# A two-block transformer kernel on one core: the gated-linear output projection and its layer norm turned to token rows, residual sums of the last projection on VectorE, two weight chunks moved in one pass

## The reference, cut to what matters

```
first_block:  x = x + g1 * rmsnorm(mixer(h));  h = rmsnorm(x)*(1+sc2)+sh2
              x = x + g2 * rmsnorm(conv_ffn(h))
layer 0:      y = (o * silu(g)) @ gla_w_out          # (256 x 1024) @ (1024 x 1024)
              x = layer_norm(ALPHA * x + y, ln_g[0], ln_b[0])
layer 1:      k, v = shared_kv(x);  y = dilated_mixer(x, k, v)    # ends with @ swa_w_out
              x = layer_norm(ALPHA * x + y, ln_g[1], ln_b[1])
```

## Time and profile before

| | us |
|---|---|
| median of three runs (785.42 to 787.11) | 786.86 |
| the profiled execution, its time | 786.95 |
| its span in the trace | 785.2 |
| PE busy, of the span | 751.5 (96%) |
| DVE busy | 528.7 (67%) |
| ACT busy | 394.9 (50%) |
| POOL busy | 121.3 (15%) |
| moved by the transfers, in all | 140.10 MB, mean 178 GB/s |

### The profile page before, as it was taken

One profiled execution on the slowest core, in us unless ns is written; L12 is line 12 of the kernel. 1 busy time (PEld: TensorE's weight loads), 2 busy tenths in 40 slices (PEclk: granted clock), 3 DMA queues, 4 the chain that ended last, 5 costly groups with the idle time before them and its releaser, 6 DMA issues. The chain is left out here.

```text
span 785.2 us, 14371 instructions
## 1 busy us (share of the span) xinstructions
PE 751.5 (96%) x6044; PEld 732.4 (93%) x6044; DVE 528.7 (67%) x770; ACT 394.9 (50%) x555; POOL 121.3 (15%) x100
## 2 busy tenths in 40 slices
PE   8899989999898999999999999999989999999996
PEld 7889889899897999999999999999989999999995
DVE  5879978765868687778656556926685556556544
ACT  4195454555353555454444347627445555555633
POOL 0040000000521100000002150000025655333000
PEclk9999999999999999999999999979999999999999
DMA  8975575464355356554565524523437653333101
GB/s 355 417 291 215 215 268 187 190 259 171 108 177 199 115 208 210 173 200 157 209 247 210 211 90 180 184 88 108 145 124 246 201 185 135 134 109 119 44 1 54
DMA packets 20954, 140.10 MB, mean 178 GB/s; under 512 B 2357, under 2 KB 2997, under 8 KB 4890
## 3 DMA queue, kind: packets, MB, share of 16 engines
q1 hardware_dynamic: 20458, 137.28, 48.2%
q0 software_dynamic: 432, 1.90, 0.7%
HBM read 138.12 MB, written 1.05 MB: 177 GB/s over the span
## 5 line engine op out<-in xcount | busy, mean ns | idle before, releaser
L1593 PE MATMUL res<-hhi,whi 128*128 128x256 f32 (+1 forms) x1120 | 322.9, 288 | 5.3 <-DVE hlo L1071 2.9
L1035 DVE TENSOR_TENSOR wlo<-raw,whi 128x2048 fp32r<-128x2048 f32 (+3 forms) x102 | 230.0, 2256 | 142.9 <-ACT whi L647 138.3
L1595 PE MATMUL res<-hlo,whi 128*128 128x256 f32 (+1 forms) x1120 | 317.8, 284 | 0.0
L1594 PE MATMUL res<-hhi,wlo 128*128 128x256 f32 (+1 forms) x1120 | 317.8, 284 | 0.0
L647 ACT ACTIVATE whi<-raw 128x2048 fp32r<-128x2048 f32 (+3 forms) x102 | 190.1, 1865 | 132.5 <-issue 100.2
L1593 PEld LDWEIGHTS res<-hhi,whi 128*128 128x128 f32 (+1 forms) x1120 | 214.6, 192 | 7.2 <-issue 5.5
L1594 PEld LDWEIGHTS res<-hhi,wlo 128*128 128x128 f32 (+1 forms) x1120 | 214.4, 191 | 0.3
L1595 PEld LDWEIGHTS res<-hlo,whi 128*128 128x128 f32 (+1 forms) x1120 | 214.3, 191 | 0.2
L559 POOL TENSOR_TENSOR sq<-sq 128x512 f32<-128x512 f32 x6 | 14.9, 2482 | 293.7 <-ACT sq L853 168.5
L1593 PE MATMUL res<-uhi,whi 128*128 128x256 f32 x176 | 49.3, 280 | 1.0 <-ACT y L854 1.0
L1594 PE MATMUL res<-uhi,wlo 128*128 128x256 f32 x176 | 49.2, 280 | 0.0
(11 more groups left out here) (331 smaller groups left out, 1242.0 us busy)
## 6 DMA issues: line engine op xcount, KB each, us to landing
raw<-in_wts SPq DMA_DIRECT2D x97, 1024.0 KB, 4.9
raw<-in_w_ada SPq DMA_DIRECT2D x16, 1024.0 KB, 4.9
shared<-in_w_ada SPq DMA_DIRECT2D x6, 1024.0 KB, 12.6
gates<-in_wts SPq DMA_DIRECT2D x3, 1024.0 KB, 15.4
raw<-in_wts SPq DMA_DIRECT2D x4, 768.0 KB, 7.3
y<-in_w_ada SPq DMA_DIRECT2D x2, 1024.0 KB, 10.3
x<-in_xT SPq DMA_DIRECT2D x2, 512.0 KB, 4.5
ln_rows<-in_ln_rows POOLq DMA_DIRECT2D x1, 1024.0 KB, 7.9
```

Of the source, the lines that this page charges most:

```text
L1035: nc.vector.tensor_tensor(lo[:, 0:b], raw[RAW_OF["w", c] % RAW][:, 0:b], hi[:, 0:b].bitcast(f32), ALU.subtract).then_inc(lo_ready, 1)
L1593: mm(out, ah, bh, start=first, stop=False)
L1594: mm(out, al, bh, start=False, stop=False)
L1595: return mm(out, ah, bl, start=False, stop=last)
```

## The change

1. The output projection of the gated-linear layer is token-major. `GOUT` is one narrow product for both halves of the tokens; then for each half t of 128 tokens comes a wide product, in which the stationary activations stay and the 512 columns of two chunks (`GOUT+1`, `GOUT+2`, slots 0 and 2 of one `whi` tensor) move in one pass, and a narrow one (`GOUT+3`, split into a buffer of its own, `wgo`). PE adds the residual from `xe` by identity matmuls.
2. The norm n5 is made on rows (`rows_centred`, `rows_scaled`), and PE then turns the rows back (`hidden(t)`: 8 transposes). ACT and DVE split them into `hhi`, `hlo` (`hidden_high`, `hidden_low`). `SK` and `SK+1` are then products of their own (`fm`) in place of one interleaved `fm_first`. POOL loads `ln_rows5` (1 MB).
3. The last projection: wide product for `SOUT`, `SOUT+1`; `SOUT+2` and `SOUT+3` in quarter results; the residual is added by DVE as it reads the result (`row_add`), PE's identity matmuls there are gone.
4. n2, n3, n4: all additions to `x` on DVE, `ada` of `UP` after the n2 additions in place of ahead of them, `load_root()` earlier on ACT (at `WOUT+2` and `DOWN`), in n4 the low parts are made between the additions, and 24 fillers in place of 36.

```diff
@@ ACT
                 if b not in LATE and b not in (GOUT + 1, GOUT + 2) and b != WOUT + 2 and b >= DIRECT:
                     high(c + 2)
...
+                if b == DOWN:
+                    load_root()
...
                     if j == 2:
+                        load_root()
                         high(c + 2)
...
+                if b == GOUT + 3:
+                    row_sum(result(FIRST_RESULT[b])[:, :], 1, T, 512, 1).then_inc(drained_act, 1)
+                    act.wait_ge(z_shift, 2)
+                    row_squares(z[:, 1, 0:768], 1, 0, 3).then_inc(z_squared, 1)
+                    hidden_high(0)
+                    high(SK)
+                    ps = result(FIRST_RESULT[b] + 1)[:, 0:T]
+                    row_sum(ps, 1, 768, T, 2).then_inc(z_summed, 1)
+                    row_squares(ps, 1, 768, 4).then_inc(drained_act, 1)
+                    row_root(1, 0)
+                    hidden_high(1)
+                    high(SK + 1)
@@ DVE, n2 and n4
-                            if i == 1 and k % 2:
-                                ins.then_inc(y_scaled[n], 1)
-                            else:
-                                own(ins)
-                        if i != 1:
-                            nc.vector.tensor_tensor(x[:, 2 * j:2 * j + 2, :], x[:, 2 * j:2 * j + 2, :],
-                                                    y[:, 2 * j:2 * j + 2, :], ALU.add).then_inc(scaled[n], 1)
-                        if n == "n4" and i == 2:
-                            low_pair(0)
+                            own(ins)
+                        if n == "n4" and i:
+                            low_pair(i - 1)
+                        nc.vector.tensor_tensor(x[:, 2 * j:2 * j + 2, :], x[:, 2 * j:2 * j + 2, :],
+                                                y[:, 2 * j:2 * j + 2, :], ALU.add).then_inc(scaled[n], 1)
                     if n == "n4":
-                        for i in (1, 2, 3):
-                            low_pair(i)
+                        low_pair(3)
                 if b == UP - 1:
+                    ada(ADA_AFTER[UP])
@@ DVE, the rows
+                if b == GOUT + 3:
+                    dve.wait_ge(drained_act, RESULT_DRAIN[FIRST_RESULT[b]][1])
+                    shift_of(1)
+                    hidden_low(0)
+                    low(SK)
+                    rows_centred(1, 0, gv)
+                    rows_scaled(1, 0, gv, x_rows, x_rows_ready)
+                    hidden_low(1)
+                    low(SK + 1)
...
+                def row_add(ps, t, a, n, at):
+                    return nc.vector.tensor_tensor_reduce(out=z[:, t, a:a + n], in0=ps, in1=x_rows[:, t, a:a + n], op0=ALU.add,
+                                                          op1=ALU.add, scale=1.0, scalar=0.0, accum_out=zs[:, t, at:at + 1])
@@ PE
-                        warm(36)
+                        warm(24)
...
+            def wide_product(ps, t, k, ih, il, slots, first, last):
+                wh, wl = (h[:, slots, k * T:k * T + T] for h in (whi, wlo))
+                return three(ps[:, :].rearrange("p (s n) -> p s n", s=2), ih[:, k, t * P:t * P + P], il[:, k, t * P:t * P + P],
+                             wh, wl, first, last)
...
+                    if c == GOUT:
+                        pe.wait_ge(xe_ready, 1)
+                        ps = bank(r)
+                        for t in range(2):
+                            residual(ps, T * t, t, (0, 1))
+                        wh, wl = weights(c)
+                        for k in range(KT):
+                            pe.wait_ge(go_lo, k // 2 + 1)
+                            for t in range(2):
+                                last = token_product(ps, T * t, t, k, gohi, golo, wh, wl, False, k == KT - 1 and t == 1)
+                        last.then_inc(product_done, 1)
+                    if c == GOUT + 1:
+                        for t in range(2):
+                            ps = bank(r + 1 + 2 * t)
+                            residual(ps, 0, t, range(2, 6))
+                            wait_weights(GOUT + 2)
+                            for k in range(KT):
+                                last = wide_product(ps, t, k, gohi, golo, slice(0, 3, 2), False, k == KT - 1)
+                            last.then_inc(product_done, 1)
+                            if t == 1:
+                                hidden(0)
+                            ps = bank(r + 2 + 2 * t)
+                            residual(ps, 0, t, (6, 7))
+                            wh, wl = weights(GOUT + 3)
+                            for k in range(KT):
+                                last = token_product(ps, 0, t, k, gohi, golo, wh, wl, False, k == KT - 1)
+                            last.then_inc(product_done, 1)
+                        warm(16, ident, pX[:, 0:P])
+                        hidden(1)
```

More of the change, by code:

```diff
@@ L102, in drainer_of @@
         return "dve"
-    if GOUT <= c < SV or SWA <= c < SWA + 12:
+    if SK <= c < SV or SWA <= c < SWA + 12 or c >= SOUT:
         return "dve"
@@ L130 @@
     CHUNK_MARK.append(_m)
+CHUNK_MARK[GOUT + 1] = RESULT_MARK[FIRST_RESULT[GOUT + 3]]
+CHUNK_MARK[GOUT + 2] = CHUNK_MARK[GOUT + 1]
 STREAM = []
@@ L197, in laid_out @@
     if c < SK:
-        return cols(gla_out, 256 * (c - GOUT), 256)
+        return cols(gla_out, (0, 512, 256, 768)[c - GOUT], 256)
     if c < SWA:
@@ L220, in build @@
         raw = [sb(f"raw{i}", [P, CW]) for i in range(RAW)]
-        whi = [sb(f"whi{i}", [P, CW], f32r) for i in range(SPL)]
-        wlo = [sb(f"wlo{i}", [P, CW], f32r) for i in range(SPL)]
+        whi = sb("whi", [P, SPL, CW], f32r)
+        wlo = sb("wlo", [P, SPL, CW], f32r)
         hhi = sb("hhi", [P, KT, T], f32r)
@@ L712, in _ @@
                     nc.scalar.activation(alrT[:, :], ps[0:16, 0:T], ACT.Copy).then_inc(drained_act, 1)
-                if b not in LATE and b != WOUT + 2 and b >= DIRECT:
+                if b == DOWN:
+                    load_root()
+                if b not in LATE and b not in (GOUT + 1, GOUT + 2) and b != WOUT + 2 and b >= DIRECT:
                     high(c + 2)
@@ L931, in _ @@
                         nc.scalar.activation(gohi[:, 2 * i:2 * i + 2, :], y[:, 2 * i:2 * i + 2, :], ACT.Copy).then_inc(go_hi, 1)
-                if GOUT < b < SK:
-                    n, j = "n5", b - GOUT
-                    for i in ((), (0, 1), (2,), (3,))[j]:
-                        act.wait_ge(centered[n], i + 1)
-                        nc.scalar.activation(sq[:, 2 * i:2 * i + 2, :], tb[:, 2 * i:2 * i + 2, :], ACT.Square
-                                             ).then_inc(squares[n], 1)
-                    if j == 2:
-                        load_root()
@@ L949, in _ @@
                     act_count[0] += 1
+                    load_root()
+                if b == GOUT + 1:
+                    row_sum(result(FIRST_RESULT[b])[:, :], 0, T, 512, 1).then_inc(drained_act, 1)
+                    act.wait_ge(z_shift, 1)
+                    row_squares(z[:, 0, 0:768], 0, 0, 3).then_inc(z_squared, 1)
+                if b == GOUT + 2:
+                    ps = result(FIRST_RESULT[b])[:, 0:T]
+                    row_sum(ps, 0, 768, T, 2).then_inc(z_summed, 1)
+                    row_squares(ps, 0, 768, 4).then_inc(drained_act, 1)
+                    row_root(0, 0)
@@ L950, in _ @@
                 if b == SOUT + 1:
                     load_root()
-                    for t in range(2):
-                        act.wait_ge(z_shift, t + 1)
-                        nc.scalar.activation(w[:, t, 0:512], z[:, t, 0:512], ACT.Square, bias=zs[:, t, 5:6],
-                                             accum_out=zs[:, t, 3:4]).then_inc(z_squared, 1)
                 if b >= SOUT + 2:
                     t = b - SOUT - 2
-                    ps = result(FIRST_RESULT[b])
-                    nc.scalar.activation(z[:, t, 512:1024], ps[:, :], ACT.Copy, accum_out=zs[:, t, 2:3]).then_inc(z_summed, 1)
@@ L1265, in _ @@
                     unit_slot(2 * (c - ZG))
-                if b + 2 in ADA_AFTER and b != WOUT:
+                if b + 2 in ADA_AFTER and b not in (WOUT, UP - 2):
                     ada(ADA_AFTER[b + 2])
@@ L1516, in _, with hidden_low @@
                         half = slice(512 * i, 512 * i + 512)
-                        nc.vector.scalar_tensor_tensor(result_rows[:, t, half], w[:, t, half], r, b_row[:, half],
-                                                       ALU.mult, ALU.add).then_inc(out_ready, 1)
+                        nc.vector.scalar_tensor_tensor(dst[:, t, half], w[:, t, half], r, b_row[:, half], ALU.mult, ALU.add
+                                                       ).then_inc(ready, 1)
+                def hidden_low(t):
+                    for i in range(2):
+                        dve.wait_ge(h_hi, 2 * t + i + 1)
+                        ks, ts = slice(4 * i, 4 * i + 4), slice(t * P, t * P + P)
```

(2 more changed lines are left out.)

328 lines of the change are left out of this document (136 added, 192 removed).

## The result

| | before | changed kernel |
|---|---|---|
| median of the runs | 786.34 us (785.42 to 787.11, 4) | 779.38 us (778.78 to 779.78, 4) |
| profiled execution: time, span | 786.95, 785.2 us | 779.67, 777.9 us |

The ratio is 0.9911, with a 95% interval of 0.9894 to 0.9929: 7.0 us faster, where 7.45 was forecast. Executions of one kernel lie 1 to 3.5 us apart here, so I compare places inside a stage, not sums, wherever a term is meant.

A forecast was written before the change was run, and what follows sets the result against it. PE, busy for 96% of the span, was taken to bound the kernel. From the profiled 786.95: -2.35 - 1.0 - 2.55 + 2.2 + 1.65 - 5.4 = -7.45, so 779.5 us; range 776.5 to 783.5.

The forecast's parts named there:

- n2/n3: Norms near 235 us: n2 starts 2.6 us earlier, the moved reductions overrun DVE's hole by 0.3; -2.35 us.
- `DOWN`: At `DOWN`, PE's wait for ACT's first copy goes because the table load stands two chunks earlier; -1.0 us.
- n4: Norm near 445 us: fewer fillers and earlier low parts let PE start `GK` sooner; -2.55 us.
- low clock at attention: Small attention matmuls near 500 us: the prediction had no term for a clock fall there.
- gated-linear projection: From 550 us to `SK`: last product 2.9 us later, row norm queued badly on DVE, `SK` later; +2.2 us.
- clock at `SK`: Longer PE standing ahead of `SK` drops the clock, its first 3.3 us at half speed; +1.65 us.
- last projection: At the end: products start earlier, wide products cheaper, PE's residual records gone, tail on DVE; -5.4 us.
- the ACT step: ACT's table load moved off the last squares ahead of n2; if it gave nothing, n2/n3 would be -1.2 us.
- Half the columns move more cheaply (-0.95): Gated-linear projection: wide matmuls of 512 columns at 0.22 us against narrow ones at 0.12; -0.95 us.
- rivals 4 and 5: Wide matmuls: 4, 0.13 us each, 771, chance 0.03; 5, off the one-pass rate, 0.43 each, 799.6, chance 0.06.
- The queue: Ahead of n5's second half, DVE stands in `low(SK)` though the row sums are there; 1.9 us lost.
- Rival 3: Gains at n2, `DOWN` and n4 are taken back by a later PE wait; 785.4, chance 0.07.

The follow-up runs named there:

- Experiment 6: Changed kernel with the two reductions and the small product for n3 put back ahead of n2 on DVE; 780.45 us, ratio 0.9927.
- experiment 7: Changed kernel with 36 fillers at n4 instead of 24; 780.41 us, ratio 0.9930.
- after: The changed kernel itself, with the whole change against the kernel before; 779.38 us, ratio 0.9911.
- 12: Kernel of 11 with the small attention matmuls spread twice as thin, in sixteen groups of four, half of them in the chunk before; 770.87 us, ratio 0.9793.
- 2: Changed kernel with the weight split of `SK` moved earlier on ACT and DVE, ahead of the first half's low part on DVE; 776.09 us, ratio 0.9871.
- experiment 3: Kernel of 2 with the first half's second low part moved behind the second half's row norm on DVE; 775.8 us, ratio 0.9872.
- 1: Changed kernel with 30 filler matmuls instead of 16 behind the last gated-linear product; 777.94 us, ratio 0.9886.
- 9: Kernel of experiment 5 plus the changed last projection, x turned by 16 transposes on PE, gated-linear projection and n5 as before; 776.65 us, ratio 0.9867.
- experiment 4: Changed kernel with each of the 96 wide matmuls made as two of 256 columns; 779.56 us, ratio 0.9912.
- 11: Changed kernel with the edits of experiment 3 and experiment 10 together; 773.46 us, ratio 0.9833.
- experiment 5: Kernel before with only the change's parts at n2/n3, `DOWN` and n4; 780.89 us, ratio 0.9924.
- 8: Changed kernel with the last projection's residual added on PE by six float32 identity matmuls, DVE adding a zero column; 783.34 us, ratio 0.9962.
- experiment 10: Changed kernel with the small attention matmuls spread behind the k steps of the next chunk's first half; 780.32 us, ratio 0.9904.

## Why the prediction was right, and where it was not

| step | predicted | its place in the trace | undone or alone |
|---|---|---|---|
| n2/n3 | -2.35 | -2.64 | 2.6 at the place (6) |
| `DOWN` | -1.0 | -1.04 | not undone alone |
| n4 | -2.55 | -2.40 | 2.3 at the place (7) |
| low clock at attention | 0 | +1.27 | full-speed time lost: 5.15 us before, 6.85 after, 3.45 (7), 0 (12) |
| gated-linear projection | +2.2 | +2.94 | 1.9 taken back by order (2, 3) |
| clock at `SK` | +1.65 | +1.41 | 1.4 (1) |
| last projection | -5.4 | -5.40 | -5.4 (9) |

- *The norms.* All three steps are right at their places. n2 started 2.73 us earlier (2.6 predicted), and from n2 to n3 it takes 10.68 us against 10.59: the reductions overran the hole by 0.26 (2.65 us in it, from 242.98 to 245.63, against 2.39), as predicted, but the scalings and additions, counted even, took 0.17 less. Experiment 6 put the reductions alone back and lost 2.6 us, so the ACT step and the additions on DVE give nothing without them. Of n4's two halves, experiment 7 undid the fillers alone, and that was enough to lose all but 0.1 us of it; the reverse was not tried. `DOWN` rests on its place in the trace alone.
- *Gated-linear projection.* The mechanism is right, the size 0.7 us too small. From the last product to `SK` it takes 9.24 us, where 9.2 was written; so all of the error lies ahead of that. The last product ends later than computed (fillers start at 573.55, which is 3.5 us later in the stage than before, where 2.9 was written): wide matmuls took 0.233, not 0.22, which is 0.6 us over 48. The step that failed is "Half the columns move more cheaply (-0.95)". They do not: experiment 4 puts two narrow ones 0.003 above one wide, which makes 0.16 us of the 0.95. The Trainium skill, "TensorE: Matmul & The Clock Gate", section "Back-to-back issue gap", names about 131 ns for 512 columns in such a stream; measured here it is 233 ns, and the measurement decides. So rivals 4 and 5 both fell: they would have needed 0.13 us or 0.43 us.
- *The queue.* `low(SK)` ahead of the second norm cost what the rows said, 1.9 us, of which experiments 2 and 3 took back 1.28 and 0.61.
- *The clock at `SK`.* It fell, and filling the hole (1) removed it. The term was 0.24 us too large: matmuls slow down from 0.12 to 0.21 us, not to twice 0.12. The row that it was read from is weaker than it looked: where PE stands 1.8 us ahead of 106 us, two of the five profiles with that hole have the low stretch behind it and three don't. That a hole of this size alone decides is not shown: with holes of 1.5 us the clock stayed up in experiment 3 and was low in the profiled executions of 11 and 12, 3.4 us each (at 574 to 578 us in 12). With 2.1 to 2.2 us it stayed up in all four (before, 2, 5, 9), with 3.35 us it was low in all six profiles that have it.
- *Last projection.* All of its 5.4 us is there, and 9 shows that it needs the rows of x but nothing else of the new gated-linear stage. That the sum is exact is luck, since its terms were off both ways: the earlier start gave 4.10 (3.95 written), the eight later records 0.81 (0.9), the wide products 0.3 at most (0.9; experiment 4 makes it 0.16), and the tail, counted as a loss of 0.35, gave 0.21.
- *The sum.* The terms that were counted come to -7.13 in place of -7.45: 0.74 too much hope at the gated-linear projection, taken back in part by the clock (0.24) and n2/n3 (0.29). Two things that were not in the sum cancel in the profiled pair, -1.43 us ahead of n2 and +1.27 at the attention block, most of them scatter of single executions. So the mechanism was right, and the nearness of the total is in part luck.
- *Rival 3.* It was partly true, but by another way than it said. Of the 6.2 us of the norms, experiment 5's profile loses 1.35 at the attention block; and experiments 6 and 7, which come to it later, lose 1.3 us less in it than the commoner reading. It is not a wait, as I had written, but the length of a low-clock stretch. Why it depends on the moment at which PE comes to it, or whether it scatters by itself, stays open: after and experiments 5, 8 and 9 reach `GK` within 0.14 us of each other, and their profiles lose 6.8, 6.8, 5.1 and 5.1 us of full-speed time.

## What to carry to other kernels

Read the granted clock over the whole program before pricing an edit, not only at its place: a stretch of many small matmuls can lose more than all the waits of a tuned norm, and what earlier work gained can be given back there. Here it paid to spread such matmuls thinly between large ones; half as thinly it did not (experiments 12 and 10). When a layout change moves work to a new norm, look first at which large copy stands ahead of the small late operation in the same engine's queue; here its place was worth 1.9 us, and the low clock behind the hole another 1.4.

## What was unexpected in the hardware

- The attention block pulled the granted clock down although PE was busy all along: in the changed kernel 0.89 of the us from 498, every us in full from 499 on, and the clock falls behind 500. Spread over the first half of one chunk, the clock fell in some executions and not in others (774.75 to 782.15 us); spread over twice the length it was 1.00 there in the profiled one, and five executions lay within 1.6 us.
- The small matmuls of 16 columns take about 0.063 us a record ahead of the fall (48 start from 506.1 to 509.2 us in the kernel before) and about 0.095 behind it (81 start from 500.7 to 508.4 in the changed one). That is 1.5 times as long at half the clock, where a product matmul of 256 columns takes 1.8 times as long (0.21 against 0.12 us). The 0.053 in the expectation of experiment 10 counted 19 records to the us from 499, but three of these began before it; and its 0.086 is the mean of the block over both levels (10.81 us for 125 records). Their difference, which is what its sum used, comes out all the same.
- One matmul of 512 columns costs the same as two of 256: 0.2335 against 2 x 0.118 us, although it loads its stationary operand once and not twice (5916 weight loads in the changed kernel, 6012 in experiment 4).
- PE stood 1.8 us ahead of 106 us in five profiles; in two of them a low stretch of 3.4 us followed, in three none.
